# Stick-breaking stage: value products over stacked high and low halves, and the logits copied by ScalarE

## What is computed

```python
z = einsum('bhqd,bhkd->bhqk', q, k) * 64 ** -0.5
causal = key_pos[None, :] < q_pos[:, None]
log_beta = log_sigmoid(z)
log_keep = where(causal, log_beta - z, 0.0)
between = cumsum(log_keep, axis=3, reverse=True) - log_keep
w = where(causal, exp(log_beta + between), 0.0)
out = einsum('bhqk,bhkd->bhqd', w, v)
```

## Time and profile before

| what | value |
|---|---|
| median of 3 runs | 3494.41 us (3491.72 to 3497.82) |
| profiled execution | 3497.59 us, its span 3495.8 us |
| PE busy over the span | 3112.3 us, 89% |
| DVE busy | 1773.6 us, 51% |
| ACT busy | 1186.1 us, 34% |
| POOL busy | 1089.1 us, 31% |
| the stage | from 92.72 us (first absolute value) to 471.05 us (last `av` matmul) |

### The profile page before, as it was taken

How to read it: one execution, slowest core, us unless ns; L and a number is a source line. 1 busy time by engine, 2 the same in 40 slices (tenths; PEclk the granted TensorE clock), 3 DMA queues, 4 the chain that set the end, 5 groups by cost and what they waited for, 6 DMA issues and landing times.

```text
span 3495.8 us, 36734 instructions
## 1 busy us (share of the span) xinstructions
PE 3112.3 (89%) x14488; PEld 2568.4 (73%) x14488; DVE 1773.6 (51%) x1804; ACT 1186.1 (34%) x1880; POOL 1089.1 (31%) x426
## 2 busy tenths in 40 slices
PE   5888789999989999999887898899976689999997
PEld 4666568887878888888676677688855567777786
DVE  5788843112253444444666334577744746656533
ACT  2666720001131000000322223577742425555511
POOL 2111024444424444444345232111122022121152
PEclk9999999999999999999887898999997889999998
DMA  2000021112211111111112111200031110000131
GB/s 94 19 25 31 19 90 48 49 49 68 71 31 49 49 49 49 49 49 49 43 49 102 37 67 52 79 31 25 31 126 37 55 36 25 31 25 31 55 115 67
DMA packets 44572, 178.99 MB, mean 51 GB/s; under 512 B 4672, under 2 KB 5696, under 8 KB 43392
## 3 DMA queue, kind: packets, MB, share of 16 engines
q1 hardware_dynamic: 32976, 119.89, 10.8%
q10 hardware_dynamic: 11440, 56.89, 4.2%
HBM read 147.40 MB, written 29.36 MB: 51 GB/s over the span
## 4 chain that ended last, share of the span: by engine, by line
PE 71%; DVE 10%; issue 10%; ACT 5%; POOL 2%; DMA 1%; SPq 0%; ACTq 0%; DVEq 0%; POOLq 0%
PE ps L456 47%; PE ps L1022 4%; PE aux L933 3%; PE ps L872 2%; PE ps L917 2%; PE ps L576 1%; PE ob L500 1%; PE ps L478 1%; PE ob L952 1%; PE ob L955 1%; PE ob L953 1%; POOL wh L413 1%; PE aux L935 1%; DVE zb L1789 1%; PE aux L605 1%
## 5 line engine op out<-in xcount | busy, mean ns | idle before, releaser
L413 POOL TENSOR_TENSOR wh<-raw,con 128x1024 fp32r<-128x1024 f32 x211 | 512.8, 2430 | 2345.5 <-PE ps L456 1209.4
L415 POOL TENSOR_TENSOR wl<-raw,wh 128x1024 fp32r<-128x1024 f32 x211 | 576.2, 2731 | 16.5
L456 PE MATMUL ps<-hh,wh 128*128 128x512 f32 x1536 | 480.2, 394 | 29.1 <-POOL wl L415 11.4
L456 PE MATMUL ps<-hl,wh 128*128 128x512 f32 x1536 | 477.8, 392 | 0.0
L456 PE MATMUL ps<-hh,wl 128*128 128x512 f32 x1536 | 476.6, 392 | 0.0
L456 PEld LDWEIGHTS ps<-hh,wh 128*128 128x128 f32 x1536 | 290.4, 190 | 92.2 <-issue 18.4
L456 PEld LDWEIGHTS ps<-hl,wh 128*128 128x128 f32 x1536 | 291.4, 190 | 61.5
L456 PEld LDWEIGHTS ps<-hh,wl 128*128 128x128 f32 x1536 | 291.1, 190 | 61.3
L1669 DVE TENSOR_TENSOR px_l<-px,px_h 128x512 fp32r<-128x512 f32 (+3 forms) x288 | 214.1, 745 | 115.6 <-ACT px_h L1526 113.4
L1911 DVE TENSOR_TENSOR y_t<-y_t,ps 128x1024 f32<-128x1024 f32 x120 | 146.5, 1221 | 174.5 <-PE ps L456 174.5
L1259 ACT ACTIVATE ff<-fr 128x1024 f32<-128x1024 f32 x32 | 33.9, 1061 | 552.9 <-DVE fr L1900 552.9
(11 more groups left out here) (353 smaller groups left out, 6299.2 us busy)
## 6 DMA issues: line engine op xcount, KB each, us to landing
raw<-wall SPq DMA_DIRECT2D x211, 512.0 KB, 3.5
spill_x<-x_t ACTq DMA_DIRECT2D x2, 4096.0 KB, 12.7
spill_out<-ot ACTq DMA_DIRECT2D x16, 512.0 KB, 2.6
go<-spill_out ACTq DMA_DIRECT2D x16, 512.0 KB, 5.9
xold_t<-spill_x ACTq DMA_DIRECT2D x2, 4096.0 KB, 16.4
x_t<-xt SPq DMA_DIRECT2D x8, 512.0 KB, 8.7
spill_o<-op ACTq DMA_DIRECT2D x4, 1024.0 KB, 3.8
o_all<-spill_o ACTq DMA_DIRECT2D x2, 2048.0 KB, 11.5
```

What stands on the lines that cost most here:

```text
L413: pool.tensor_tensor(wh[:, s, :, :], raw[:, s, :, :], ones.unsqueeze(1).broadcast_to([P, KT, P]), ALU.mult).then_inc(w_high, 1)
L415: pool.tensor_tensor(wl[:, s, :, :], raw[:, s, :, :], wh[:, s, :, :].bitcast(F32), ALU.subtract).then_inc(w_split, 1)
L456: m = pe.matmul(ps[:, w, a:b], lw[:, sl, k, :], r[:, i, a:b], start=(i == 0 and j == 0), stop=(i == len(ks) - 1 and j == 2))
```

## The change

The high and the low part of v are put side by side as 128 stationary columns (64 high, 64 low), so that one matmul gives the high part's product in the partitions 0 to 63 of `ob` and the low part's in 64 to 127. A unit and head then has two matmuls (by `pw_h`, by `pw_l`) instead of three; the product of low by low comes with it. At the end of a chunk the two halves of `ob` are added: ACT copies the upper halves into a new tile `op_sum`, DVE adds the lower halves to it, and one step later ACT makes `op_h` and DVE `op_l` from `op_sum`. The loop on ACT and DVE has one step more. PE's first `av` of a chunk waits for `osum_ready` instead of `o_ready`.

The copy of the logits of unit s into `zb` goes from DVE (after the softplus) to ACT, between Exp of `zb` and Exp of `eb`; its wait for `av_done` goes with it.

```diff
-                for a, r in ((0, pw_h), (1, pw_h), (0, pw_l[u % 3])):
-                    m = pe.matmul(ob[0:64, h, first:first + n], v[a][:, kb, h * 64:(h + 1) * 64], r[:, h, 0:n],
+                for r in (pw_h, pw_l[u % 3]):
+                    m = pe.matmul(ob[:, h, first:first + n], v[:, kb, h, :, :].rearrange("p a f -> p (a f)"), r[:, h, 0:n],
                                   start=False, stop=True, skip_group_check=True)
...
-        for step in range(NU + 4):
+        for step in range(NU + 5):
...
             if a < NU:
+
+                if a >= 3:
+                    act.wait_ge(av_done, a - 2)
+                copy(zb[a % 3][:, :, 0:n], zsrc[:, :, 0:n]).then_inc(z_free, 1)
                 act.wait_ge(abs_ready, a + 1)
                 act.activation(e, e, ACT.Exp, scale=-1.0).then_inc(ea_ready, 1)
...
+                copy(op_sum[LO, cols], ob[HI, 0, :])
+                copy(op_sum[HI, cols], ob[HI, 1, :]).then_inc(olow_ready, 1)
+            late = step - 4
+            if 0 <= late < NU and SB_UNITS[late][2] == 0:
+                pair, chunk = SB_UNITS[late][0:2]
                 cols = slice(chunk * HALF, (chunk + 1) * HALF)
-                copy(op_h[LO, cols], ob[0:64, 0, :])
-                copy(op_h[HI, cols], ob[0:64, 1, :]).then_inc(oh_ready, 1)
+                act.wait_ge(osum_ready, 2 * pair + chunk + 1)
+                copy(op_h[:, cols], op_sum[:, cols]).then_inc(oh_ready, 1)
...
-            if a < NU:
-                n = SB_UNITS[a][4]
-                dve.wait_ge(abs_ready, a + 1)
-
-                if a >= 3:
-                    dve.wait_ge(av_done, a - 2)
-                zsrc = ps[:, Z_SLOT, :].rearrange("p (h q) -> p h q", h=2)
-                dve.tensor_copy(zb[a % 3][:, :, 0:n], zsrc[:, :, 0:n]).then_inc(z_free, 1)
...
+                dve.wait_ge(olow_ready, 2 * pair + chunk + 1)
+                dve.tensor_tensor(op_sum[LO, cols], ob[0:64, 0, :], op_sum[LO, cols], ALU.add)
+                dve.tensor_tensor(op_sum[HI, cols], ob[0:64, 1, :], op_sum[HI, cols], ALU.add).then_inc(osum_ready, 1)
+            late = step - 4
+            if 0 <= late < NU and SB_UNITS[late][2] == 0:
+                pair, chunk = SB_UNITS[late][0:2]
+                cols = slice(chunk * HALF, (chunk + 1) * HALF)
                 dve.wait_ge(oh_ready, t.next(oh_ready))
-                cols = slice(chunk * HALF, (chunk + 1) * HALF)
-                low(op_l[LO, cols], ob[0:64, 0, :], op_h[LO, cols])
-                low(op_l[HI, cols], ob[0:64, 1, :], op_h[HI, cols]).then_inc(o_ready, 1)
+                low(op_l[:, cols], op_sum[:, cols], op_h[:, cols]).then_inc(o_ready, 1)
```

More of the change, by code:

```diff
@@ L151, in program @@
     ks = [(at(2 + 2 * i, f"k_h{i}", [P, S], F32R), at(3 + 2 * i, f"k_l{i}", [P, S], F32R)) for i in range(2)]
-    vs = [(at(u, f"v_h{u}", [P, 8, P], F32R), at(u + 1, f"v_l{u}", [P, 8, P], F32R)) for u in (6, 16)]
+    vs = [at(u, f"v_hl{u}", [P, 8, 2, 2, 64], F32R) for u in (6, 16)]
     vts = [at(u, f"vt{u}", [P, S], F32) for u in (6, 16)]
@@ L156, in program @@
     op_h, op_l = op[:, 0, :], op[:, 1, :]
+    op_sum = at(1, "op_sum", [P, S], F32)
     zb = [at(18 + i, f"zb{i}", [P, 2, HALF], F32) for i in range(3)]
@@ L257, in program @@
     tri_done, d_ready, pwh_ready, pwl_ready = map(sem, ("tri_done", "d_ready", "pwh_ready", "pwl_ready"))
-    av_done, oh_ready, o_ready = map(sem, ("av_done", "oh_ready", "o_ready"))
+    av_done, olow_ready, osum_ready, oh_ready, o_ready = \
+        map(sem, ("av_done", "olow_ready", "osum_ready", "oh_ready", "o_ready"))
     abs_ready, ea_ready, pw_ready, rest_done = map(sem, ("abs_ready", "ea_ready", "pw_ready", "rest_done"))
@@ L619, in av @@
                 if t.now("chunks") > 0:
-                    pe.wait_ge(o_ready, t.now("chunks"))
+                    pe.wait_ge(osum_ready, t.now("chunks"))
                 t.take("chunks")
@@ L1153, in sb_take @@
             else:
-                copy(vs[pair % 2][0][:, :, :], ps[:, slot, :].rearrange("p (k f) -> p k f", k=8)).then_inc(high_ready, 1)
+                copy(vs[pair % 2][:, :, :, 0, :], ps[:, slot, :].rearrange("p (k h f) -> p k h f", k=8, h=2)).then_inc(high_ready, 1)
         for piece in ("q", "k", "v", "vt"):
@@ L1199, in _ @@
                     act.wait_ge(op_left, 16 * pair)
+                copy(op_sum[LO, cols], ob[HI, 0, :])
[3 more added lines that the diff above has]
+                pair, chunk = SB_UNITS[late][0:2]
                 cols = slice(chunk * HALF, (chunk + 1) * HALF)
-                copy(op_h[LO, cols], ob[0:64, 0, :])
-                copy(op_h[HI, cols], ob[0:64, 1, :]).then_inc(oh_ready, 1)
-            sent = step - 4
+                act.wait_ge(osum_ready, 2 * pair + chunk + 1)
+                copy(op_h[:, cols], op_sum[:, cols]).then_inc(oh_ready, 1)
+            sent = step - 5
             if 0 <= sent < NU and SB_UNITS[sent][1:3] == (1, 0):
@@ L1776, in sb_take @@
             else:
-                low(vs[pair % 2][1][:, :, :], ps[:, slot, :].rearrange("p (k f) -> p k f", k=8),
-                    vs[pair % 2][0][:, :, :]).then_inc(free, 1)
+                low(vs[pair % 2][:, :, :, 1, :], ps[:, slot, :].rearrange("p (k h f) -> p k h f", k=8, h=2),
+                    vs[pair % 2][:, :, :, 0, :]).then_inc(free, 1)
         for piece in ("q", "k", "v", "vt"):
@@ L1826, in _ @@
             if 0 <= done < NU and SB_UNITS[done][2] == 0:
-                chunk = SB_UNITS[done][1]
+                pair, chunk = SB_UNITS[done][0:2]
+                cols = slice(chunk * HALF, (chunk + 1) * HALF)
+                dve.wait_ge(olow_ready, 2 * pair + chunk + 1)
[4 more added lines that the diff above has]
+                pair, chunk = SB_UNITS[late][0:2]
+                cols = slice(chunk * HALF, (chunk + 1) * HALF)
                 dve.wait_ge(oh_ready, t.next(oh_ready))
-                cols = slice(chunk * HALF, (chunk + 1) * HALF)
-                low(op_l[LO, cols], ob[0:64, 0, :], op_h[LO, cols])
-                low(op_l[HI, cols], ob[0:64, 1, :], op_h[HI, cols]).then_inc(o_ready, 1)
+                low(op_l[:, cols], op_sum[:, cols], op_h[:, cols]).then_inc(o_ready, 1)
             piece, _, tiles, pair, number = sb_piece(step)
```

## The result

| | before | changed |
|---|---|---|
| median | 3493.9 us (4 runs, 3491.7 to 3497.8) | 3520.4 us (4 runs, 3514.6 to 3525.1) |
| span of the profiled execution | 3495.8 us | 3518.9 us |

The ratio is 1.0069, 95% interval 1.0057 to 1.0082: slower by 0.7%, 26.5 us in the medians and 23.1 us in the profiled executions. The forecast was 3516 us, +21.7; the interval stands for 20 to 29 us, so its size lies inside what was measured.

The account below looks back on a forecast made before the run. The stage was bound by each step's ring of waits, no engine being full. Terms 3.6 + 5.3 + 5.0 + 6.3 + 2.8 + 0.3 - 0.9 - 0.7 gave +21.7 us, hence 3516 us, range 3497 to 3532.

Parts of the forecast that it names:

- The ring: Each step's loop subtraction, ACT, DVE, PE, subtraction; its longest way sets the step, 6.76 us full-width in the last pair.
- Rival (a): Busiest engine, DVE, sets the stage; losing 48 us of copies there makes the kernel faster, 3476 us; chance 0.13.
- items 1 to 5: Wide last-pair steps +3.6, projection-copy ends +5.3, chunk ends +5.0, steps after them +6.3, others on ACT's way +2.8 us.
- item 3: Seven steps in which a chunk ends: the 768-column logits' copy adds 0.71 us each, +5.0 us together.
- q's steps: Steps 4, 16, 28, counted with 40: `sp_h` waits for the mask anyway, taking back half; 0.25 us each.
- The new work at a chunk's end: Step after a chunk's end: Ln, logits' copy 0.92, `op_h` 0.6, low part 0.7 before the subtraction; step 39 +1.7 us.
- item 6: Nine steps with a POOL split: held `pw_l` covers the later `sp_h`, +0.3 us; without that some 6 us.
- The savings of PE: 96 fewer `av` matmuls, 20 us of PE time, mostly off the path: -0.9 behind POOL splits, -0.7 at the last `av`.
- item 4: Steps after the seven chunk ends: `op_h` copy and low part stand ahead of the next subtraction, +6.3 us.
- Rival (c): The ring lengthens as forecast and PE's clock falls too: +5 to +15 us on top, 3528 us; chance 0.13.
- DVE idle for about 1.7 us before `sp_l`: Sign expected in a full-width step of the last pair, with 7.7 us between subtractions instead of 6.76.
- no wait of PE's logits for the copy in the last pair: Sign expected in the changed profile: the earlier 13.2 us of such waits, ten times, would be gone.

Follow-up runs that it names:

- e5: The changed kernel with the logits copied twice on ScalarE, one after the other in the same place: 3556.7 us, ratio 1.0180.
- e2: The changed kernel with the logits' copy back on VectorE, so the stacked value product and its sums alone: 3503.8 us, ratio 1.0024.
- e1: The kernel before with only the logits' copy moved to ScalarE, three value matmuls kept: 3515.2 us, ratio 1.0059.
- e7: The changed kernel with POOL splitting only 2 of 8 tiles after the first two slabs, the rest left out: 3430.1 us, ratio 0.9817.
- e4: The changed kernel with the `op_h` copy before the wait for `d_ready` and the `op_l` part after the softplus: 3517.9 us, ratio 1.0063.
- e6: The kernel before with POOL splitting only 2 of 8 tiles after the first two slabs, the rest left out: 3405.3 us, ratio 0.9746.
- e11: The changed kernel with the logits' copy on VectorE and one extra zero-weight matmul per unit and head: 3498.7 us, ratio 1.0010.
- e8: The changed kernel with the logits' copy on VectorE, `op_h` copy before the `d_ready` wait and `op_l` after the softplus: 3498.8 us, ratio 1.0015.
- e12: The changed kernel with one extra zero-weight matmul per unit and head, logits' copy on ScalarE: 3518.7 us, ratio 1.0066.
- e10: The kernel before with only ScalarE's copy to `sp_h` taken earlier where unit s-1 is off the diagonal: 3497.5 us, ratio 1.0011.
- e9: The changed kernel with ScalarE's copy to `sp_h` ahead of the logits' copy where unit s-1 is off the diagonal: 3517.6 us, ratio 1.0075.
- e3: The changed kernel with ScalarE's logits' copy straight after the absolute value, before the wait for `d_ready`: 3515.4 us, ratio 1.0055.

## Why the prediction was right, and where it was off

The direction, the mechanism and the size came out. Point by point:

- **The ring, not the busiest engine.** Rival (a) said the stage follows DVE. DVE lost 10.8 of its 81.7 us in the second pair and the pair grew by 6. e5 doubles the copy and each step on ScalarE's way round pays it again. What carried the forecast was one reading: `sp_l` had idle time before it, the copy on DVE did not end last.
- **Step by step.** The items 1 to 5 sum to 23.1 us against 23.0 forecast; none is off by more than 0.6. That they meet so closely is in part luck: in item 3 a step that paid nothing and one that paid 0.35 more for a lower clock stand beside five that paid 0.12 more than the 0.71 forecast, for the new copies and additions (0.14 in e2), which the forecast had put at nothing. A whole copy (0.90) where ACT is on the path, less where the mask was waited for anyway (q's steps +0.13 instead of 0.25), nothing where PE's projection or POOL's hold is longer. e1 shows that the copy alone costs 21 us, most of the 26.5.
- **The new work at a chunk's end** was sized by Ln + copy + `op_h` + low part: +1.7 for step 39, measured 2.05. In it the copy waits 0.34 us for the value product, which the forecast had put at nothing; the granted clock in this step was 0.50. e7, with 0.76 there, pays 1.59. e4 takes that late part off the end and gets 4.0 us back in those steps.
- **The cover of item 6 holds**, all but in step 17 (+0.61, and +0.60 in e1), but it was put down to POOL alone; e6 and e7 show that PE stands just behind it. The "some 6 us" without POOL's hold was wrong: it is 1.1 us.
- **The savings of PE.** The forecast had them off the path but for 1.6 us, and they were: 1.0 us came. Beside item 4 and item 3 it put the stacked product's cost at nothing. That term was mis-sized: e2 alone costs 9.6 us in the medians and 4.5 in the steps. About 0.8 us is the chunk ends and 1.1 is step 39; 3 us are the steps 41 and 44 without anything new, in a stretch where the granted clock is 0.81 instead of 0.94. That the clock makes those two longer is borne out by e11 (41) and e8 (44), which have 1.00 there and lose nothing.
- **Rival (c)** was right in this much: the clock fell, in the last pair from 0.94 to 0.83. The forecast weighed it as an alternative at 5 to 15 us, where it is a part of the same case and much cheaper. In the change its marks are step 14 (0.35 us over e12's, which had 1.00 there) and step 48 (+0.67 at 0.76, and 0.00 in e12 at 0.83), about 1 us; e12 as a whole gives 0.8 us of steps back. A low mean clock does not always lengthen a step: e1's step 48 had 0.76 too and lost nothing.
- **Signs that failed.** The forecast wanted DVE idle for about 1.7 us before `sp_l`; it is 2.79, because the sum added the copy on ACT and forgot that DVE's own copy of 1.22 us leaves its place empty. It wanted no wait of PE's logits for the copy in the last pair; 5.8 us are left. Neither was in the sum of the time.
- **What stays open.** Some 3 to 5 us of e2 lie after the stage (the trace's shift is +4.2 at the end of the MLP and +7.2 at the end of the program). In the other direction e1's trace has +23.4 at the end of the MLP and +16.8 at the end of the program, and e10's median is 2.9 us slower with the steps only 1.0 longer. No run separates what is stacking there and what differs from one execution or one kernel to the next.

No version here that does the whole work beats the kernel before (e6 and e7 leave three quarters of POOL's split out). e8 and e11 are the nearest with the stacked product, 5 us slower.

## What to carry to other kernels

In a software pipeline over several engines find for each kind of step which instruction ends the wait of the next one, and move work only off that ring; an engine's busy share (83% here) is no reason to unload it, and an engine at 68% is no place to load if every one of its instructions stands ahead of the hand-over. A moved instruction lengthens each hand-over behind it in the in-order queue, not just the first: look for the second lane (`pw_h`) before reordering. Matmuls taken off PE in a stretch where it waits for others are worth nearly nothing there, and may cost granted clock. And before reading a step's length look at the clock granted in that step.

## What had not been expected of the hardware

- In the profiled executions PE's granted clock went down with the number of its matmuls. In the last pair it was 0.94, 0.93, 0.96 and 0.90 with six value matmuls a unit (before, e1, e6, e10); 0.83, 0.81, 0.86, 0.91, 0.75, 0.82, 0.88 and 0.79 with four stacked ones (the change, e2 to e5, e7 to e9); 0.90 and 0.89 with four and two more by zero (e11, e12). It is one execution for each kernel, and e4 with 0.91 stands above e10 with 0.90, so the clock also moves with the rest of the step or by chance.
- Where PE's granted clock over a step was 1.00 in both traces and nothing in the step was changed, the step repeats from kernel to kernel to about 0.02 us (step 13: 8.59, 8.57, 8.58, 8.58 in before, the change, e1, e2). The large exceptions lie in steps in which the clock was lower in one of the two: step 2 (6.81 us at 1.00; 8.68, 8.96, 8.96 and 8.95 at 0.68, 0.66, 0.81 and 0.81 in e1, e3, e4, e9), 43 in e10, 44 in e2. So single steps tell what the medians, whose runs spread over 4 to 12 us, cannot.
- POOL's split of weights is dear far beyond this stage: a quarter of it (e6, which leaves three quarters out) makes the whole program 88.5 us faster. By its trace 14.7 us of that lie up to the first convolution multiply (1.3 of them before the first subtraction, where the traces differ anyway), 1.4 in the convolution, mixing and MLP that follow, and the rest in the attention stages behind 1650 us.
